# Turns and bias rows of the expert blocks done as pairs of 64-column fp32 products

## The chip, the cores and the metric

The kernel runs on one core of one Trainium2 chip. The metric is device time of one execution in microseconds (us), the median of several runs. Lower is better. The profile is one further execution, taken by the hardware profiler.

## The reference, cut to what matters

One layer of a decoder (a mixer of pooling, convolution and a recurrent unit, then a mixture of experts) is applied to 520 tokens of width 1024. The change lies in the mixture of experts:

```python
logits = (xt @ router_w + router_b)
top_v, top_i = lax.top_k(logits, TOP_K)          # 4 of 32 experts for each token
...
g = xblk @ w_gate[e] + b_gate[e]                 # 1024 x 1024 each, fp32
u = xblk @ w_up[e] + b_up[e]
g = jnp.minimum(g, SWIGLU_LIMIT)
u = jnp.clip(u, -SWIGLU_LIMIT, SWIGLU_LIMIT)
glu = g * jax.nn.sigmoid(SWIGLU_ALPHA * g)
((u + 1.0) * glu) @ w_down[e] + b_down[e]
...
y = jax.ops.segment_sum(yb * row_w[:, None], row_tok, num_segments=T + 1)[:T]
```

All 32 experts are visited. Each has three matrices of 4 MiB, so 384 MiB of weights are read from HBM in one execution.

## The kernel before, in words

The first 300 us or so compute the mixer, the router and the tables that say which tokens go to which expert. The rest, up to about 1298 us, is the loop over experts, `for s in range(E)` on each engine, and a tail that sums up the output.

**Blocks.** An expert has 64, 96, 128 or 160 places for tokens, by its rank in size: `WIDTH[s]` is 2 (20 experts), 3 (6 experts), 4 (4 experts) or 5 (2 experts). `BLOCKS` cuts them into blocks of 64 and 32 places: (64,), (64, 32), (64, 64), (64, 64, 32).

**Products (L1893 to L1898).** A block of 64 places uses the TensorE array as two halves of 64 columns. The places are the stationary operand, 512 columns of weights the moving one. Half 0 makes output columns 0 to 511 on partitions 0 to 63, half 1 makes 512 to 1023 on partitions 64 to 127, so that one PSUM bank holds 64 places by 1024 outputs. A block of 32 places uses four quarters of 32 columns in the same way, 256 moving columns each. Everything is plain fp32. In `project` a matrix takes four chunks of 1 MiB with two steps of 128 rows each, so a 64-place block makes 4 x 2 x 2 = 16 calls of `mm`.

**Other fp32 `mm` calls named below.** The router (L1823) makes 8 calls for a tile of 128 tokens: 128 columns of `h2T` stationary, 32 columns of `rw` moving. The conditioning products (L1626) put the 9 columns of `cT` on four column quarters, with 128 moving columns each, in 32 calls for a group.

**Bias rows (`bias`, L1884).** Each accumulation begins with the bias: `sel` (128x128, fp32r) has in its columns a one at the row of this expert's bias in `btab` (128x512, fp32r). For a 64-place block this is one product over the full 128 columns of the array. For a 32-place block it is four 32-column fp32 products (L1891).

**Turns.** The gathered rows (`xrow`, token by feature) are turned to feature by token by `turn_rows`, eight transposes of 128 columns with `ident` as moving operand (L1570). 24 gathers are turned, 16 of 128 rows, 6 of 96 and 2 of 32. The activations `act_t` are turned by `turn_act` before the down projection: 4 transposes for each 64-place block, 2 for each 32-place block, 168 in all. The banks of turned rows are copied to SBUF by ScalarE and VectorE.

**Order on TensorE, for each s.** Gate project, up project, turn of the rows of the next expert (where a new gather is due), down of expert s-1, turn of the activations of s.

**Loads.** SyncE loads the weights in order, in chunks of 1 MiB, into a ring of 18 buffers. A load waits until TensorE has finished with the chunk that lay in its buffer (`m_used`). All of it is in one hardware queue. Gathers (of `xrow`) and scatters (of the results) go through GpSimd.

Of the kernel before, what the change touches and what calls it, by code (L numbers as in the profile page):

```python
# [5 lines left out]
F32 = mybir.dt.float32  # L6
# [8 lines left out]
P = 128  # L15
D = 1024
KC = D // P
# [47 lines left out]
T_BANKS = (6, 7, 4)  # L65
# [49 lines left out]
def trunk_program(nc, x_prompt, x_sample, state_pool, state_conv, state_lru_conv, state_lru_h, c_prompt, c_sample,  # L115
# [36 lines left out]
    (hT_hi, hT_lo), W0 = place(A0, ("hT_hi", [P, KC, TOK], F32R), ("hT_lo", [P, KC, TOK], F32R))  # L152

    (oT, oS, _), OEND = place(A0, ("oT", [P, TT - 1, 2, KC, P], F32R), ("oS", [P, KC, NB], F32), ("oS_pad", [P, KC, NB], F32))
    assert OEND <= W0
    (scr1,), _ = place(A0, ("scr1", [P, D], F32))
# [67 lines left out]
    (acc, out_t, sq_e), T1 = place(0, ("acc", [P, 2, D], F32), ("out_t", [P, TT, D], F32), ("sq_e", [P, D], F32))  # L224
    (yrow_a,), G1 = place(A0, ("yrow_a", [P, 2, K, D], F32))
    (_, yrow_b), G2 = place(N0, ("xrow_pad", [P, 2, D], F32), ("yrow_b", [P, 3, K, D], F32))
    assert G2 <= M2
    TAIL = (TT - 1,) + tuple(range(TT - 1))
# [10 lines left out]
    with ctx:  # L239
        psum = ctx.enter_context(nc.psum_tensor("psum", [P, 8, 512], F32))  # L240
        bk = [psum[:, i, :] for i in range(8)]
# [314 lines left out]
        def _(g):  # L556
# [142 lines left out]
            for s in range(E):  # L699
                for n, _, _, _ in TURNS[s + 1]:  # L700
                    g.wait_ge(xt_ps, n + 1)
                    if n + 2 < ALL_TURNS:
                        gather(n + 2)
                if s:
                    scatter(s - 1)
# [854 lines left out]
        def _(pe):  # L1560
            mm = nc.tensor.matmul
# [7 lines left out]
            def turn(out, src, rows):  # L1569
                return nc.tensor.transpose(out, src, ident[0:rows, 0:rows])  # L1570
# [4 lines left out]
            for k in range(KC):  # L1575
                last = turn(bk[4][:, NC * k:NC * k + NC], c_all[:, k * P:k * P + P], NC)
# [60 lines left out]
            for m in range(16):  # L1637
                last = turn(bk[2][:, NC * m:NC * m + NC], modA[:, m * P:m * P + P], NC)
# [4 lines left out]
            for k in range(KC):  # L1643
                last = turn(bk[5][:, NB * k:NB * k + NB], x1[0:NB, TT - 1, k * P:k * P + P], NB)
            last.then_inc(xs_ps, 1)
            for k in range(KC):
                if k >= 2:
                    pe.wait_ge(h1_act, k - 1)
                for t in range(TT - 1):
                    last = turn(bk[3 + k % 2][:, t * P:t * P + P], x1[:, t, k * P:k * P + P], P)  # L1650
# [112 lines left out]
            for m in range(4):  # L1763
                turn(bk[1][0:11, m * P:m * P + P], x_lru[:, m, LB + SEQ - LB:LB + TOK], P)
                last = turn(bk[2][0:9, m * P:m * P + P], h_tail[:, m, :], P)
# [77 lines left out]
            for b in range(1, TT):  # L1843
                last = mm(bk[5][:, E * b:TT * E], ones_b[:, :], mask[:, 0:TT - b, :].rearrange("p t e -> p (t e)"),
                          start=False, stop=(b == TT - 1))
# [3 lines left out]
            for b in range(TT):  # L1849
                last = mm(bk[7][0:E, 256:256 + E], mask[:, b, :], ones_b[:, 0:E], start=(b == 0), stop=(b == TT - 1))  # L1850
# [3 lines left out]
            for e in range(2):  # L1854
                for t in range(TT):
                    last = mm(bk[1][0:FIRST, 2 * e:2 * e + 2], hot01[:, 2 * t + e, :], spots[:, t, :], start=(t == 0),
                              stop=(t == TT - 1))
# [7 lines left out]
            def find_rows():  # L1865
# [4 lines left out]
                              start=(i == 0), stop=(i == TT * K - 1))  # L1870
                last.then_inc(idx_ps, 1)

            def turn_rows(b, rows, full, evicted, count):

                pe.wait_ge(x_rows[b], full)
                if evicted is not None:
                    pe.wait_ge(aT_a, evicted)
                    pe.wait_ge(xg_a, count)
                    pe.wait_ge(xg_d, count)
                for k in range(KC):  # L1880
                    last = turn(bk[6 + k // 4][:, (k % 4) * P:(k % 4) * P + rows], xrow[0:rows, b, k:D:KC], rows)
                last.then_inc(xt_ps, 1)

            def bias(out, mat, w):  # L1884

                if w == 64:
                    mm(out, sel[:, :], btab[:, mat, :], start=True, stop=False)  # L1887
                else:
                    for g4 in range(4):
                        h, c = g4 // 2, 256 * (g4 % 2)  # L1890
                        mm(out[32 * g4:32 * g4 + 32, :], sel[:, 64 * h:64 * h + 32].bitcast(F32),  # L1891
                           btab[:, mat, c:c + 256].bitcast(F32), start=True, stop=False)
# [38 lines left out]
            def turn_act(widths):  # L1931

                for b, w in enumerate(widths):
                    for j in range(w // 16):
                        last = turn(bk[T_BANKS[b]][:, P * j:P * j + P], act_t[:, b, 256 * (j // 2) + j % 2:256 * (j // 2) + 256:2], P)
                    last.then_inc(at_ps, 1)

            def parts_of(s):
# [6 lines left out]
            def full_at(c0):  # L1945
                return lambda j: 16 * ((c0 + j) // NBUF + 1)

            turn_rows(0, GATHERS[0][1], 16, None, None)
            for s in range(E):
                c0, widths, before = first_chunk(s), BLOCKS[WIDTH[s]], blocks_before(s)  # L1950
                pe.wait_ge(sel_done, s + 1)
                pe.wait_ge(xg_a, turns_before(s))
                pe.wait_ge(xg_d, turns_before(s))
                if s >= 3:
                    pe.wait_ge(y_a, blocks_before(s - 2))
                project(0, [bank_of(G_BANKS, s, b) for b in range(len(widths))], widths, parts_of(s), c0, full_at(c0))
                if s == 0:
                    find_rows()
                if s >= 2:
                    pe.wait_ge(y_a, blocks_before(s - 1))  # L1960
                if s:
                    pe.wait_ge(aT_a, before)
                project(1, [bank_of(U_BANKS, s, b) for b in range(len(widths))], widths, parts_of(s), c0 + 4, full_at(c0 + 4))
                for n, _, rows, _ in TURNS[s + 1]:
                    turn_rows(n % 2, rows, 16 * (n // 2 + 1), before if before else None, n)
                if s == 1:
                    pe.wait_ge(tables_done, 1)
                if s:
                    pe.wait_ge(glu_done, before + len(widths))
                    down([down_bank(s - 1, b) for b in range(len(BLOCKS[WIDTH[s - 1]]))], BLOCKS[WIDTH[s - 1]],  # L1970
                         c0 + 8, full_at(c0 + 8))
                pe.wait_ge(act_done, before + len(widths))
                pe.wait_ge(xg_a, turns_before(s + 1))
                pe.wait_ge(xg_d, turns_before(s + 1))
                turn_act(widths)
            for t in range(TT):
                out = bk[0][0:E, t * P:t * P + P] if t < 4 else bk[1][0:E, 0:P]
                last = turn(out, wfull[:, t, :], P)
# [6 lines left out]
            def extra(q):  # L1985

                def full(c):
                    def count(j):
                        slot = (12 + c + j) % NBUF
                        return q * 16 + 16 * (-(-(12 * E - slot) // NBUF) + 1)  # L1990
                    return count

                pe.wait_ge(y_a, q * 2 + ALL_BLOCKS)
                turn_rows(0, P, q * 16 + 16 * (len(range(0, ALL_TURNS, 2)) + 1), q * 2 + ALL_BLOCKS, q + ALL_TURNS)
                pe.wait_ge(xg_a, q + (ALL_TURNS + 1))
                pe.wait_ge(xg_d, q + (ALL_TURNS + 1))
                pe.wait_ge(sel_done, q + (E + 1))
                both = [(xa, 0), (xa, 64)]
                project(0, (bk[4], bk[5]), (64, 64), both, 12, full(0))
                project(1, (bk[0], bk[1]), (64, 64), both, 16, full(4))  # L2000
                pe.wait_ge(act_done, q * 2 + (ALL_BLOCKS + 2))
                turn_act((64, 64))
                pe.wait_ge(aT_a, q * 2 + (ALL_BLOCKS + 2))
                down((bk[2], bk[3]), (64, 64), 20, full(8))
# [5 lines left out]
            def tail_out_banks(i):  # L2010

                return [bk[2 * (i % 4) + n][0:ROWS[TAIL[i]], :] for n in range(2)]
# [16 lines left out]
            for i, t in enumerate(TAIL):  # L2029
# [6 lines left out]
                for n in range(2):  # L2036
                    for j in range(BY_PE[i]):
                        last = mm(tail_out_banks(i)[n], diag[0:r, i, j, 0:r], yrow[i][0:r, j, 512 * n:512 * n + 512],
                                  start=False, stop=(j == BY_PE[i] - 1))
# [29 lines left out]
```

## Time and profile before

| | |
|---|---|
| median of 3 runs | 1357.33 us (1352.21 to 1359.2) |
| the profiled execution | 1352.83 us |
| its span in the profile | 1351.1 us |
| TensorE (PE) busy | 1256.2 us, 93% |
| TensorE weight load (PEld) busy | 560.7 us, 41% |
| VectorE, ScalarE, GpSimd busy | 21%, 15%, 8% |
| read from HBM | 470.26 MB |
| mean granted TensorE clock | 0.967 of full speed |

The busy time of TensorE is the union of its matmuls, each drawn with its pipeline latency, so that a run of matmuls is best measured from its start to the start of the next. "x64" behind a row is a count of instructions as the chip ran them.

### The profile page before, as it was taken

The page shows a single profiled execution, that of the slowest core. Times are in us where ns is not written, and L with a number is a line of the kernel's source. Part 1 is how long each engine was busy: PE and PEld are TensorE (multiplying, and loading weights), DVE is VectorE, ACT ScalarE, POOL GpSimd, SP SyncE. Part 2 cuts the span into 40 slices and gives each one's busy share as a digit, 9 for nine tenths or more (in the row PEclk, how much of TensorE's full clock was granted, in tenths as well). Part 3 has the DMA queues.
Part 4 walks back from the last instruction along what each step waited for, and adds up shares of the span by engine and source line. Part 5 has one row for each costly group of instructions (what it writes and reads, how often), then busy time and mean ns, then how long its engine had stood idle before and what let it go on. Part 6 is the DMA issues. An engine that isn't in the chain of part 4 may idle for free.

```text
span 1351.1 us, 19196 instructions
## 1 busy us (share of the span) xinstructions
PE 1256.2 (93%) x8190; PEld 560.7 (41%) x8190; DVE 287.0 (21%) x562; ACT 198.4 (15%) x347; POOL 110.4 (8%) x176
## 2 busy tenths in 40 slices
PE   2899977968999999999999999999999999999976
PEld 1686955843333333333333333333333333333322
DVE  0651585576100100000000000001001010001027
ACT  3513243220010000000000001001001000100012
POOL 3010022010000000100001100000001001000000
PEclk9999988968999999999999999999999999999978
DMA  9551479379999999999999999999999999999974
GB/s 317 194 160 32 156 246 350 138 312 403 348 403 420 421 422 421 408 409 422 407 407 420 420 415 421 421 420 403 419 417 420 421 421 421 420 422 421 422 299 183
DMA packets 95076, 486.43 MB, mean 360 GB/s; under 512 B 13649, under 2 KB 21852, under 8 KB 45302
## 3 DMA queue, kind: packets, MB, share of 16 engines
q1 hardware_dynamic: 83306, 461.15, 84.9%
q0 software_dynamic: 8608, 20.82, 4.1%
q10 hardware_dynamic: 3076, 3.22, 0.8%
q8 instruction: 66, 1.08, 0.3%
q14 instruction: 20, 0.16, 0.0%
HBM read 470.26 MB, written 18.04 MB: 361 GB/s over the span
## 4 chain that ended last, share of the span: by engine, by line
PE 81%; DMA 8%; DVE 5%; SPq 3%; ACTq 1%; ACT 1%; issue 1%; POOL 0%; DVEq 0%; POOLq 0%
PE psum L1897 61%; PE psum L1570 5%; PE psum L1565 3%; PE psum L1566 3%; PE psum L1567 3%; DMA raw<-in_moe_w_gate 2%; DMA raw<-in_moe_w_down 2%; SPq L481 2%; PE psum L1887 2%; DMA bd_x<-in_lru_wx 1%; ACTq L755 1%; PE psum L1719 1%; DMA raw<-in_w_out 1%; PE psum L2018 1%; DMA xrow<-h_scratch,gidx 1%
## 5 line engine op out<-in xcount | busy, mean ns | idle before, releaser
L1897 PE MATMUL psum<-raw,aT 128*64 128x512 f32 (+1 forms) x1728 | 301.2, 533 | 4.0 <-DMA raw<-in_moe_w_down 3.8
L1897 PE MATMUL psum<-raw,xb 128*64 128x512 f32 (+1 forms) x1920 | 304.0, 512 | 0.3 <-DMA raw<-in_moe_w_gate 0.3
L1897 PE MATMUL psum<-raw,xa 128*64 128x512 f32 x1280 | 283.5, 595 | 0.0
L1491 DVE TENSOR_SCALAR act_t<-psum 128x512 f32<-128x512 f32 (+1 forms) x46 | 28.4, 642 | 873.5 <-PE psum L1897 873.5
L1897 PEld LDWEIGHTS psum<-raw,xb 128*64 128x64 f32 (+1 forms) x1920 | 100.4, 126 | 189.0 <-issue 175.0
L1897 PEld LDWEIGHTS psum<-raw,aT 128*64 128x64 f32 (+1 forms) x1728 | 98.3, 129 | 187.8 <-issue 166.7
L1897 PEld LDWEIGHTS psum<-raw,xa 128*64 128x64 f32 x1280 | 88.2, 137 | 169.7 <-issue 169.7
L979 ACT ACTIVATE glu<-psum 128x512 f32<-128x512 f32 (+1 forms) x46 | 24.2, 559 | 291.6 <-PE psum L1897 291.6
L661 POOL DMA_INDIRECT xrow<-h_scratch,gidx x24 | 27.5, 1145 | 464.4 <-PE psum L1570 430.4
L1565 PE MATMUL psum<-hT_hi,w_hi 128*128 128x260 f32 x208 | 59.4, 286 | 0.0
L1566 PE MATMUL psum<-hT_lo,w_hi 128*128 128x260 f32 x208 | 58.9, 283 | 0.0
L1567 PE MATMUL psum<-hT_hi,w_lo 128*128 128x260 f32 x208 | 58.7, 282 | 0.0
L673 POOL DMA_INDIRECT y_scratch<-yst_a,sunit x23 | 22.9, 997 | 305.6 <-ACT yst_a L994 260.4
L994 ACT ACTIVATE yst_a<-psum 128x512 f32<-128x512 f32 (+1 forms) x27 | 14.5, 558 | 210.3 <-PE psum L1897 210.3
L1626 PE MATMUL psum<-raw,cT 128*9 128x128 f32 x768 | 33.2, 342 | 8.9 <-DMA raw<-in_ada_w 7.3
L1565 PEld LDWEIGHTS psum<-hT_hi,w_hi 128*128 128x128 f32 x208 | 39.1, 188 | 0.9 <-issue 0.8
L1567 PEld LDWEIGHTS psum<-hT_hi,w_lo 128*128 128x128 f32 x208 | 39.2, 189 | 0.0
L1566 PEld LDWEIGHTS psum<-hT_lo,w_hi 128*128 128x128 f32 x208 | 39.1, 188 | 0.1
L1570 PE MATMUL psum<-ident,xrow 128*128 128x128 f32 (+2 forms) x192 | 27.9, 290 | 9.2 <-DMA xrow<-h_scratch,gidx 9.2
L1887 PE MATMUL psum<-btab,sel 128*128 128x512 f32 x76 | 34.3, 477 | 1.1 <-ACT xb L1004 1.1
L1570 PEld LDWEIGHTS psum<-ident,xrow 128*128 128x128 f32 (+2 forms) x192 | 23.5, 198 | 28.0 <-issue 18.7
L1570 PEld LDWEIGHTS psum<-ident,act_t 128*128 128x128 f32 x168 | 22.5, 208 | 27.0 <-issue 25.2
(399 smaller groups left out, 923.6 us busy)
## 6 DMA issues: line engine op xcount, KB each, us to landing
raw<-in_moe_w_gate SPq DMA_DIRECT2D x128, 1024.0 KB, 26.3
raw<-in_moe_w_up SPq DMA_DIRECT2D x128, 1024.0 KB, 26.9
raw<-in_moe_w_down SPq DMA_DIRECT2D x128, 1024.0 KB, 26.8
raw<-in_ada_w SPq DMA_DIRECT2D x24, 1024.0 KB, 9.2
raw<-in_w_in SPq DMA_DIRECT2D x7, 1024.0 KB, 11.6
x<-in_x_prompt SPq DMA_DIRECT2D x2, 2048.0 KB
raw<-in_w_out SPq DMA_DIRECT2D x4, 1024.0 KB, 14.4
yrow_a<-y_scratch SPq DMA_DIRECT2D x2, 2048.0 KB, 10.6
```

The lines of the kernel that those rows point to most:

```text
L481: sp.dma_start(buf(slot).rearrange("p (k n) -> p k n", k=2), src).then_inc(m_full[slot], 16)
L661: g.indirect_dma_start(out=out, out_offset=None, in_=h2_d, in_offset=bass.IndirectOffsetOnAxis(ap=index, axis=0), bounds_check=h2_last, oo ...
L673: g.indirect_dma_start(out=out, out_offset=bass.IndirectOffsetOnAxis(ap=index, axis=0), in_=src, in_offset=None, bounds_check=last, oob_is ...
L979: ac.activation(glu[:, b, 0:bank.shape[1]], bank, ACT.Gelu_apprx_sigmoid).then_inc(glu_done, 1)
L1491: v.tensor_scalar(act_t[:, b, 0:bank.shape[1]], bank, 8.0, -6.0, ALU.min, ALU.max).then_inc(u_done, 1)
L1565: mm(out, lhi, rhi, start=start, stop=False)
L1566: mm(out, lhi, rlo, start=False, stop=False)
L1567: return mm(out, llo, rhi, start=False, stop=stop)
L1570: return nc.tensor.transpose(out, src, ident[0:rows, 0:rows])
L1626: last = mm(outs[j], cT[:, 4 * kh + k, :], raw[:, slot, 512 * k + P * j:512 * k + P * j + P], start=False, stop=(kh == 1 and k == 3))
L1887: mm(out, sel[:, :], btab[:, mat, :], start=True, stop=False)
L1897: last = mm(out[w * g4:w * g4 + w, :], x, weights[:, 8 * w * g4:8 * w * g4 + 8 * w], start=start, stop=stop)
```

## The change

Three kinds of full-width work in the expert loop are done as two 64-column products side by side, like the weights' own products. The transposes of gathered rows and of activations become ordinary fp32 products with the identity as moving operand. The bias row of a 64-place block becomes two products, with `sel` and `btab` read as fp32 instead of fp32r. The 32-place bias, `find_rows`, the turn of `wfull` at the end, and everything before the expert loop stay as they are.

```diff
+            def turn_halves(out, src, rows):
+
+                for h in range(2):
+                    last = mm(out[64 * h:64 * h + 64, :], src[:, 64 * h:64 * h + 64], ident[0:rows, 0:rows],
+                              start=True, stop=True)
+                return last
+
...
                 for k in range(KC):
-                    last = turn(bk[6 + k // 4][:, (k % 4) * P:(k % 4) * P + rows], xrow[0:rows, b, k:D:KC], rows)
+                    last = turn_halves(bk[6 + k // 4][:, (k % 4) * P:(k % 4) * P + rows], xrow[0:rows, b, k:D:KC], rows)
                 last.then_inc(xt_ps, 1)
...
                 if w == 64:
-                    mm(out, sel[:, :], btab[:, mat, :], start=True, stop=False)
+                    for h in range(2):
+                        mm(out[64 * h:64 * h + 64, :], sel[:, 64 * h:64 * h + 64].bitcast(F32),
+                           btab[:, mat, :].bitcast(F32), start=True, stop=False)
...
                     for j in range(w // 16):
-                        last = turn(bk[T_BANKS[b]][:, P * j:P * j + P], act_t[:, b, 256 * (j // 2) + j % 2:256 * (j // 2) + 256:2], P)
+                        last = turn_halves(bk[T_BANKS[b]][:, P * j:P * j + P],
+                                           act_t[:, b, 256 * (j // 2) + j % 2:256 * (j // 2) + 256:2], P)
                     last.then_inc(at_ps, 1)
```

## Rows read from the trace of the kernel before

**Rows 1.** The page: busy time of each engine, share of the span, instructions.

```profile
PE 1256.2 (93%) x8190; PEld 560.7 (41%) x8190; DVE 287.0 (21%) x562; ACT 198.4 (15%) x347; POOL 110.4 (8%) x176
```

**Rows 2.** Stretches: start:end, length, busy time of each engine, clock, DMA share, GB/s.

```profile
304.00:314.00 10.00, 5.99 (x25) 2.51 (x25) 9.45 (x18) 2.15 (x3) 0.00 (x0) 0.51 1.02 363
...
340.00:345.00 5.00, 5.00 (x54) 1.98 (x54) 0.00 (x0) 0.87 (x2) 0.00 (x0) 1.00 0.80 320
...
385.00:1280.00 895.00, 893.65 (x5102) 321.35 (x5100) 67.09 (x134) 76.47 (x146) 63.57 (x61) 1.00 1.01 418
```

**Rows 3.** Waits: who waited for whom, us in total, times, longest.

```profile
PE psum L1897 <- DMA raw<-in_moe_w_down: 3.8, 5, 1.1
...
SPq L481 <- PE psum L1897: 453.6, 230, 19.0
```

**Rows 4.** The page's costliest groups: line, engine, count, busy, mean ns.

```profile
L1570 PE MATMUL psum<-ident,xrow 128*128 128x128 f32 (+2 forms) x192 | 27.9, 290 | 9.2 <-DMA xrow<-h_scratch,gidx 9.2
L1887 PE MATMUL psum<-btab,sel 128*128 128x512 f32 x76 | 34.3, 477 | 1.1 <-ACT xb L1004 1.1
...
L1570 PEld LDWEIGHTS psum<-ident,act_t 128*128 128x128 f32 x168 | 22.5, 208 | 27.0 <-issue 25.2
```

**Rows 5.** PE in order of time: start, length, group (4-wide, then 2-wide expert).

```profile
800.06 13.95 PE L1897 MATMUL psum<-raw,xb 128*64 128x512 f32 x64
813.94 0.73 PE L1887 MATMUL psum<-btab,sel 128*128 128x512 f32 x2
814.60 13.95 PE L1897 MATMUL psum<-raw,xb 128*64 128x512 f32 x64
828.49 1.16 PE L1570 MATMUL psum<-ident,xrow 128*128 128x128 f32 x8
829.58 11.12 PE L1897 MATMUL psum<-raw,aT 128*64 128x512 f32 x96
840.63 1.23 PE L1570 MATMUL psum<-ident,act_t 128*128 128x128 f32 x8
841.61 0.48 PE L1887 MATMUL psum<-btab,sel 128*128 128x512 f32 x1
842.02 7.09 PE L1897 MATMUL psum<-raw,xa 128*64 128x512 f32 x32
849.04 0.49 PE L1887 MATMUL psum<-btab,sel 128*128 128x512 f32 x1
849.46 7.09 PE L1897 MATMUL psum<-raw,xa 128*64 128x512 f32 x32
856.48 1.06 PE L1570 MATMUL psum<-ident,xrow 32*128 32x32 f32 x8
857.47 2.80 PE L1897 MATMUL psum<-raw,aT 128*64 128x512 f32 x12
```

**Rows 6.** Weight loads (PEld) in order of time inside such a product run.

```profile
810.41 0.14 PEld L1897 LDWEIGHTS psum<-raw,xb 128*64 128x64 f32 x2 [0.28 <-issue]
...
812.99 0.14 PEld L1897 LDWEIGHTS psum<-raw,xb 128*64 128x64 f32 x2 [0.28 <-issue]
```

**Rows 7.** PE in order of time: small-column groups of other stages, at full clock.

```profile
188.90 1.93 PE L1626 MATMUL psum<-raw,cT 128*9 128x128 f32 x64
190.76 0.40 PE L1620 MATMUL psum<-adab,bsel 12*9 12x128 f32 x8
...
255.68 1.87 PE L1823 MATMUL psum<-rw,h2T 128*128 128x32 f32 x16
257.38 1.07 PE L1570 MATMUL psum<-ident,h2f 128*128 128x128 f32 x8
```

**Rows 8.** PE in order of time: a 3-wide expert's bias, turn of 96 rows.

```profile
701.08 0.64 PE L1891 MATMUL psum<-btab,sel 128*32 128x256 f32 x8
...
712.70 1.13 PE L1570 MATMUL psum<-ident,xrow 96*128 96x96 f32 x8
713.75 6.53 PE L1897 MATMUL psum<-raw,aT 128*64 128x512 f32 x52
```

## The prediction

> **What bounds the kernel now.** I read the page first: PE is busy 93% of the span, no other engine over 41% [rows 1]. Then the stretches: from 385 to 1280 us, which is nearly the whole expert loop, PE is busy 893.65 of 895 us and at the same time the DMA engines are at a share of 1.01 with 418 GB/s [rows 2]. Two resources are full at once, and the question is which has slack. The waits tell: PE waits for weights 3.8 us in all, in five waits, while SyncE waits 453.6 us for PE to give buffers back [rows 3]. Last, the order of time: a 64-instruction product run takes 13.88 us from its start to the start of what follows, both times that it stands there [rows 5], and its weight loads come every 0.43 us to the hundredth (six steps in 2.58 us) [rows 6], so no wait hides inside the busy time. The reader should see that each side has a slack of a few us only: if TensorE's work shrinks, the loads stay the limit. If it grows, everything over 3.8 us goes into the end.
>
> **How many instructions a call is.** An ordinary fp32 `mm` is two instructions on PE, a transpose or an fp32r product one. The router's 8 calls stand as x16 and the 32-place bias's 4 calls as x8 [rows 7, 8], and the 16 calls of a 64-place project as x32, while 8 transposes are x8 and one fp32r bias is x1 [rows 5]. A pair of halves with 512 moving columns takes 0.429 us [rows 6]; a call on both halves is two such pairs.
>
> **Bias rows.** 76 before [rows 4]. 52 stand alone (40 for the 2-wide experts, 12 for the 3-wide ones), and one takes 0.42 us from its start to the product's (849.04 to 849.46). 24 come by twos (4- and 5-wide experts), 0.66 us for both (813.94 to 814.60) [rows 5]. After: 4 instructions of 64x512 for each, two pairs of 0.429, so 0.86 us. That adds 52 x 0.44 = 22.9 and 12 x (1.72 - 0.66) = 12.7, in all 35.6 us. fp32r streams its moving columns twice as fast and in one instruction; all that is given up. The new shape is that of the products beside it, so this term is firm.
>
> **Turns.** Before, eight transposes of `xrow` take 1.09 us (828.49 to 829.58) and with 96 rows 1.05, with 32 rows 0.99; eight of `act_t` take 0.98 (840.63 to 841.61) [rows 5, 8]. So 16 x 1.09 + 6 x 1.05 + 2 x 0.99 = 25.7 us for 24 gathers (192 transposes) [rows 4] and 168 x 0.1225 = 20.6 for the activations [rows 4], 46.3 in all. After: 360 turns x 2 halves x 2 instructions = 720 pairs. No row shows a pair of 64 columns with 128 moving. The nearest is L1626: four column quarters, 128 moving, 64 instructions in 1.86 us, 0.116 for each group of four with the change of mode in it [rows 7]; a quarter of the products' 0.429 gives 0.107. From the side of the loads, the router's fp32 instructions with 128 stationary columns and only 32 moving come every 0.106 us (1.70 / 16) [rows 7]. Two loads of 64 columns can hardly cost more than one of 128, whether they run together or in turn. I take 0.111 for the 592 pairs with 128 moving columns (16 gathers and all activations), 0.10 for the 96 pairs of the 96-row gathers, 0.08 for the 32 pairs of the 32-row ones: 65.7 + 9.6 + 2.6 = 77.9, so +31.6 us. Lower bound, streaming alone: 592 x 0.107 + 96 x 0.082 + 32 x 0.055 = 73.0, +26.7. Upper bound 0.120 for all 720, a little above what the strided transposes of `act_t` show (0.1225, and those load 128 columns): 86.4, +40.1.
>
> **The mode changes that go.** A product run of 64 is 32 pairs x 0.429 = 13.73 us, and takes 13.88 where full-width work follows: 0.15 for leaving the 64-column shape and coming back. There are 88 such visits (32 for the up bias, 32 for turns of activations and gate bias together, 24 for gathered rows). The 16 bias visits of the 3- and 5-wide experts still go on to a 32-column bias, so that I count 0.05 there: 72 x 0.15 + 16 x 0.05 = 11.6 us saved. The Trainium skill ("TensorEngine Tiling (Array Packing)", Key Properties) says that changing the tiling mode drains TensorE, which speaks for the change; the trace agrees, with this 0.15. The same page (Restrictions) says that column tiling shuts out the transpose mode for fp32, and "FP8 and Floating Point Precision" (TensorE Precision Notes) counts four passes for a true fp32 product, which speaks against it: as an estimate from these two pages alone a turn of 128 rows costs 4 x 128 cycles, 0.21 us, and the sum comes out near the lower bound.
>
> **The start.** The first gather's turn and the first bias fall into a stretch with a granted clock of 0.51, the lower level of 1.2 GHz [rows 2], while all the rest runs at 1.00, the level of 2.4 GHz. Their added time, 0.3 and 0.4 us as counted, is about twice as long there: +0.8 us.
>
> **The sum.** 35.6 + 31.6 - 11.6 + 0.8 = +56.4 us of TensorE. All of it is in order on the engine that never rests, and it lies beside nothing. The only cover is the 3.8 us in which PE waited for weights: with later buffer releases the loads go on ahead and these waits vanish. That leaves +52.6. With the bounds of the turns, +47.7 to +61.1. What is late next: SyncE's loads wait for PE longer, DMA falls below its full share, GpSimd's scatters follow later, and the tail starts 53 us later, unchanged. ScalarE and VectorE copy the turns out later but their results are wanted only after a project or a down of 7 us or more, except at the very first expert. The profiled execution, 1352.8, becomes 1405.4. The median of the runs before is 4.5 us above it. Runs of before are held by the memory as much as by TensorE, and those of after by TensorE alone, so I do not carry the 4.5 over in full: 1406.
>
> **The rivals.**
> *Loads that do not overlap.* If the load of each half had to wait for the matmul in flight, a pair would cost its 0.107 and about half of the router's 0.106, some 0.165, and 720 pairs 118.8 us: +41 on my sum, 1447. Against it: in the product run two loads start together every 0.43 us right in the middle of the matmul run [rows 5, 6], and transposes come every 0.1225 though their loads alone take 208 ns from start to end [rows 4]. The Trainium skill ("TensorE: Matmul & The Clock Gate", Part 3) has the rule that loads overlap with matmuls in flight only where the row groups differ; here both halves use all rows. The trace doesn't agree with that rule. But at 128 moving columns the overlap would have to be nearly perfect, and no row has this shape, so the rival keeps 7 in 100.
> *One instruction for each half, and a cover by the loads: no slower.* If products with the identity and with `sel` were one instruction each at these same rates, the new work would be half: 38.9 for the turns against 46.3, 76 x 0.43 = 32.6 for the bias rows against 29.8, less 11.6 for the modes: TensorE wins 16 us. Then the loads decide, and nearly nothing comes of it: between 340 and 380 us the DMA engines have some idle time (share 0.80 in one stretch [rows 2]), which earlier buffer releases could fill by 1 or 2 us. 1356, no change. It decides as soon as the added TensorE time is under 3.8 us. Against it stands the count x8 for four calls of the fp32 bias. 4 in 100.
> *TensorE's growth hidden in part.* The ring of 18 buffers could hide growth only where PE now waits, and it waits 3.8 us. For a result of 1380 PE would have to hold waits that the profile doesn't show. 3 in 100.
>
> **Chances and range.** Within 0.5% (6.8 us) is about what a measurement of this kernel can tell from no change. The forecast has 86 in 100, the rivals 7, 4 and 3. The forecast's own bounds give 1400 to 1414; with 3 or 4 us for the median's own scatter on either side and the mis-sized mode changes (0.10 or 0.20 instead of 0.15 moves the sum by 3.6 each way), 1395 to 1421. Slower 0.95, same 0.04, faster 0.01.
>
> **What would show it.** In the profile after: L1887 gone as 128*128 x76 and there as 128*64 x304, turns as 128*64 with 1440 instructions or near; 0.86 us from a lone bias to its product; 1.75 to 1.8 us for eight turns of 128 rows; product runs at 13.73 instead of 13.88; no wait of PE for weights after 385 us; DMA share near 0.96 instead of 1.01. The prediction is wrong if eight turns take 2.6 us (loads exposed), or if the bias has two instructions instead of four, or if PE busy grows as said and the end does not move.

## The result, and the profile after

The change makes the kernel slower: 1405.43 us (median of 4 runs, 1402.97 to 1408.31) against 1355.14 us before (4 runs, 1352.21 to 1359.2). The ratio is 1.0381, with a 95% interval of 1.0346 to 1.0416, so +50 us. Forecast were 1406 us and a range of 1395 to 1421. The profiled execution of the changed kernel took 1408.31 us (span 1406.6), the longest of its four runs, and that of before, 1352.83, is nearly the shortest of its own. Their difference of 55.5 us is therefore a few us larger than that of the medians.

The page of the changed kernel shows more busy time on PE and PEld alone, beside [rows 1]:

```profile
PE 1317.0 (94%) x9498; PEld 619.2 (44%) x9498; DVE 288.1 (20%) x562; ACT 199.8 (14%) x347; POOL 108.4 (8%) x176
...
L1895 PE MATMUL psum<-btab,sel 128*64 128x512 f32 x304 | 77.1, 599 | 1.1 <-ACT xb L1004 1.1
...
L1876 PE MATMUL psum<-ident,xrow 128*64 128x128 f32 (+2 forms) x768 | 51.2, 287 | 8.8 <-DMA xrow<-h_scratch,gidx 8.8
...
L1876 PE MATMUL psum<-ident,act_t 128*64 128x128 f32 x672 | 42.2, 273 | 0.9 <-DVE xb L1504 0.9
```

The counts are those of "two halves, two instructions each": 76 bias rows became 304 instructions, 192 and 168 transposes became 768 and 672.

In the order of time, the same experts as in [rows 5] (a 4-wide one, then a 2-wide one):

```profile
833.06 13.90 PE L1906 MATMUL psum<-raw,xb 128*64 128x512 f32 x64
846.79 1.89 PE L1895 MATMUL psum<-btab,sel 128*64 128x512 f32 x8
848.51 13.90 PE L1906 MATMUL psum<-raw,xb 128*64 128x512 f32 x64
862.24 2.12 PE L1876 MATMUL psum<-ident,xrow 128*64 128x128 f32 x32
864.19 11.07 PE L1906 MATMUL psum<-raw,aT 128*64 128x512 f32 x96
875.08 1.92 PE L1876 MATMUL psum<-ident,act_t 128*64 128x128 f32 x32
876.83 1.03 PE L1895 MATMUL psum<-btab,sel 128*64 128x512 f32 x4
877.69 7.04 PE L1906 MATMUL psum<-raw,xa 128*64 128x512 f32 x32
...
892.38 2.11 PE L1876 MATMUL psum<-ident,xrow 32*64 32x32 f32 x32
894.42 5.80 PE L1906 MATMUL psum<-raw,aT 128*64 128x512 f32 x26
```

Read each row from its start to the next start. Two bias rows take 1.72 us (846.79 to 848.51; 0.66 before), one takes 0.86 (0.42). Eight turns of 128 gathered rows take 1.95 (1.09), eight of activations 1.75 (0.98), and eight turns of only 32 rows take even 2.04 (0.99). A product run of 64 takes 13.73 instead of 13.88: the mode changes around it are gone.

The waits and the stretch that answers to [rows 2, 3]:

```profile
PE psum L1876 <- DMA xrow<-h_scratch,gidx: 8.8, 1, 8.8
PE psum L2028 <- ACT diag L1034: 3.4, 1, 3.4
PE psum L1895 <- ACT xb L1004: 1.1, 1, 1.1
PE psum L1876 <- DVE xb L1504: 0.9, 1, 0.9
```

```profile
385.00:1280.00 895.00, 895.00 (x5966) 351.17 (x5964) 61.92 (x123) 73.69 (x139) 61.34 (x60) 1.00 0.99 399
```

No wait for weights is left among PE's waits, PE is busy for all of the 895 us, and 399 GB/s are moved where it was 418.

Where the time went can be summed from the starts of all matmuls between the first turn and the last down product, each interval given to the instruction that opens it (us). The last digits are rounded, so a column can be off by 0.1:

| | before | changed kernel | difference | the prediction's term |
|---|---|---|---|---|
| 64-place bias rows | 29.9 | 67.9 | +38.0 | +35.6, and 0.4 of the start |
| turns of gathered rows | 29.2 | 49.7 | +20.5 | +14.9, and 0.4 of the start |
| turns of activations | 20.8 | 36.8 | +16.0 | +16.7 |
| 64-column weight products | 809.4 | 791.5 | -17.8 | -11.6 modes, -3.8 waits |
| all else | 101.1 | 100.8 | -0.3 | 0 |
| whole stretch | 990.4 | 1046.8 | +56.4 | +52.6 |

Ahead of this stretch the profiled execution of the changed kernel was some 3 us later, and its tail 3 to 4 us shorter.

### The profile page after: what moved, and what is told of

It is laid out like the page before. It is cut to its first block, busy times and chain, and to the rows that moved or that the text cites. A ratio compares the mean times of both kernels' runs of the same rounds, so it can differ in the third digit from the quotient of the medians.

```text
span 1406.6 us, 21812 instructions
## 1 busy us (share of the span) xinstructions
PE 1317.0 (94%) x9498; PEld 619.2 (44%) x9498; DVE 288.1 (20%) x562; ACT 199.8 (14%) x347; POOL 108.4 (8%) x176
## 4 chain that ended last, share of the span: by engine, by line
PE 88%; DVE 5%; DMA 3%; ACTq 1%; issue 1%; ACT 1%; SPq 1%; DVEq 0%; POOLq 0%
PE psum L1906 63%; PE psum L1876 6%; PE psum L1895 5%; PE psum L1565 3%; PE psum L1566 3%; PE psum L1567 3%; DMA bd_x<-in_lru_wx 1%; PE psum L1719 1%; ACTq L755 1%; DMA raw<-in_w_out 1%; PE psum L1570 1%; PE psum L2028 1%; PE psum L1900 1%; DMA xrow<-h_scratch,gidx 1%; SPq L442 1%
## 5 line engine op out<-in xcount | busy, mean ns | idle before, releaser
L1906 PEld LDWEIGHTS psum<-raw,xb 128*64 128x64 f32 (+1 forms) x1920 | 101.1, 126 | 189.5 <-issue 177.1
L1906 PEld LDWEIGHTS psum<-raw,xa 128*64 128x64 f32 x1280 | 91.9, 137 | 182.7 <-issue 182.7
L1895 PE MATMUL psum<-btab,sel 128*64 128x512 f32 x304 | 77.1, 599 | 1.1 <-ACT xb L1004 1.1
L1876 PEld LDWEIGHTS psum<-ident,xrow 128*64 128x64 f32 (+2 forms) x768 | 51.0, 213 | 21.3 <-issue 12.4
L1876 PE MATMUL psum<-ident,xrow 128*64 128x128 f32 (+2 forms) x768 | 51.2, 287 | 8.8 <-DMA xrow<-h_scratch,gidx 8.8
L1876 PEld LDWEIGHTS psum<-ident,act_t 128*64 128x64 f32 x672 | 38.9, 139 | 18.7 <-issue 17.7
L1876 PE MATMUL psum<-ident,act_t 128*64 128x128 f32 x672 | 42.2, 273 | 0.9 <-DVE xb L1504 0.9
```

The lines of the kernel that those rows point to most:

```text
L1876: last = mm(out[64 * h:64 * h + 64, :], src[:, 64 * h:64 * h + 64], ident[0:rows, 0:rows], start=True, stop=True)
L1895: mm(out[64 * h:64 * h + 64, :], sel[:, 64 * h:64 * h + 64].bitcast(F32), btab[:, mat, :].bitcast(F32), start=True, stop=False)
L1906: last = mm(out[w * g4:w * g4 + w, :], x, weights[:, 8 * w * g4:8 * w * g4 + 8 * w], start=start, stop=stop)
```

## Experiments

Medians and ratios are against the kernel before on the same chip: 1353.85 us (15 runs) for the first four, 1353.22 us (13 runs) for the last three. "Loop" is the whole stretch of the table above, from the kernel's own trace.

### One part at a time

**bias_only**: the changed kernel with both kinds of turns put back.

```diff
-                    last = turn_halves(bk[6 + k // 4][:, (k % 4) * P:(k % 4) * P + rows], xrow[0:rows, b, k:D:KC], rows)
+                    last = turn(bk[6 + k // 4][:, (k % 4) * P:(k % 4) * P + rows], xrow[0:rows, b, k:D:KC], rows)
...
-                        last = turn_halves(bk[T_BANKS[b]][:, P * j:P * j + P],
-                                           act_t[:, b, 256 * (j // 2) + j % 2:256 * (j // 2) + 256:2], P)
+                        last = turn(bk[T_BANKS[b]][:, P * j:P * j + P], act_t[:, b, 256 * (j // 2) + j % 2:256 * (j // 2) + 256:2], P)
```

> Only the bias rows of the 64-place blocks are done as two fp32 halves; the turns stay transposes. Theory (TensorE's own time goes to the end of the run): bias rows add 35.6 us, 4.0 us of mode changes go (only the up biases stand between 64-column products), 0.4 us more at the start, and 3.8 us of waits for weights vanish: +28 us. Rival (the ring of buffers hides a growth of this size): under +10 us.

Measured: 1385.87 us, ratio 1.0239 (1.0212 to 1.0265), +32 us; loop +34.8. The rival is out. The loop grew by 6.6 us more than the expected 28 (28.2 as added up). Most of it is the seam between turns and bias. With the bias in another shape than the turns before it, the turns of activations take 26.4 us in all, and 20.8 before: 5.6 more, 0.175 for each of the 32 experts. The bias rows, at 70.3 us in all, are 4.5 above their expected growth of 36.0, and the products gave back 11.4 where 7.8 was expected.

**rows_only**: of the change, `turn_rows` alone. Against the kernel before:

```diff
-                    last = turn(bk[6 + k // 4][:, (k % 4) * P:(k % 4) * P + rows], xrow[0:rows, b, k:D:KC], rows)
+                    last = turn_halves(bk[6 + k // 4][:, (k % 4) * P:(k % 4) * P + rows], xrow[0:rows, b, k:D:KC], rows)
```

> Only the turns of gathered rows are done as fp32 halves. With the turn times of the changed kernel's trace (about 1.95 us for eight, where the prediction had 1.78): 24 x 1.96 - 25.7 = +21.3, less 3.6 for the mode changes of 24 visits, plus 0.3, less 3.8 of vanished waits: +14 us. By the prediction's own price of a pair (0.111, 0.10, 0.08) it would be +8 us. Rival (hidden by the ring): under +3 us.

Measured: 1361.95 us, ratio 1.0063 (1.0045 to 1.0082), +8 us; loop +11.2. Turns of gathered rows took 49.8 us (49.7 in the changed kernel), +20.5, while the 64-column products fell by 9.0. That is more than the 3.6 of mode changes and 3.8 of waits; the part on why the prediction was right takes it up. The median agrees with the lower of the two expected numbers, but not for its reason: the price of a turn is the higher one.

**acts_only**: of the change, `turn_act` alone. Against the kernel before:

```diff
-                        last = turn(bk[T_BANKS[b]][:, P * j:P * j + P], act_t[:, b, 256 * (j // 2) + j % 2:256 * (j // 2) + 256:2], P)
+                        last = turn_halves(bk[T_BANKS[b]][:, P * j:P * j + P],
+                                           act_t[:, b, 256 * (j // 2) + j % 2:256 * (j // 2) + 256:2], P)
```

> Only the turns of the activations are done as fp32 halves. 336 pairs x 0.109 - 20.6 = +16.0 us; no mode change goes, since the gate bias behind them is still full-width; less 3.8 us of vanished waits: +12 us. Rival (hidden by the ring): under +3 us.

Measured: 1364.01 us, ratio 1.0064 (1.0043 to 1.0086), +10 us by the medians and +9 by the ratio; loop +11.4. The size is as expected, but "no mode change goes" was only half of it: a mode change moved. The product runs before the turns end 3.1 us earlier in all, since halves follow them. The same 3.1 us come back at the seam to the full-width bias, where the turns take 39.9 us in all and 36.8 in the changed kernel. So turns and seam cost 19.1 us more than the 20.8 of before, and the products 8.0 us less.

The three parts add up to 32.0 + 8.1 + 10.2 = 50.3 us by the medians, the size of the whole change. The loops add up to 57.4 against 56.4. Each part alone, though, already used up the waits, which makes the sum too small, and bias_only and acts_only each leave a seam between shapes that the whole doesn't have, which makes it too large. These two nearly cancel.

### The other direction: less work for TensorE

**before_no_bias**: the kernel before without the bias products of 64-place blocks.

```diff
                 if w == 64:
-                    mm(out, sel[:, :], btab[:, mat, :], start=True, stop=False)
+                    pass
...
-                                                    False, j == 3 and kk == 1)
+                                                    w == 64 and j == 0 and kk == 0, j == 3 and kk == 1)
```

> The kernel before without the bias products of the 64-place blocks: their first weight product starts the accumulation, so that those blocks lack b_gate and b_up. TensorE's work shrinks by 52 x 0.42 + 12 x 0.66 + 4.0 of mode changes = 33.8 us. Theory (weights come at the full rate of the DMA engines already, so a smaller TensorE cannot help): 0 to -4 us, and PE waits for weights of some 30 us appear. Rival (TensorE alone is the bound): -34 us.

Measured: 1348.85 us, ratio 0.9957 (0.9931 to 0.9982), -5 us; loop -1.6 (988.8). All 29.9 us of bias rows are gone, and the loop is nearly as long as it was. PE's waits of this kernel say where they went:

```profile
PE psum L1897 <- DMA raw<-in_moe_w_down: 15.1, 19, 2.6
...
PE psum L1897 <- DMA raw<-in_moe_w_up: 5.4, 11, 0.6
...
PE psum L1897 <- DMA raw<-in_moe_w_gate: 1.9, 3, 0.9
```

22.4 us of waits for weights stand in place of 4.1 before (the 3.8 of [rows 3] and 0.3 more for gate weights). The products' intervals, with these waits in them, grew by 23.1 us. Another 5.5 us went to the seam behind the turns of activations (26.3 us in all, 20.8 before), as in bias_only. So TensorE's own work shrank by less than the expected 33.8 us, and the waits are fewer than the expected 30. A smaller TensorE buys next to nothing here, while a larger one costs what it grows by, less the waits of before. The run is a little faster than the expected 0 to -4 us. What is over the loop's 1.6 us lies ahead of the loop (1.1 us) and in the tail (1.9) of the profiled run, and I can't explain it by the change.

### Halves or plain fp32: which of them costs?

**bias_full_fp32**: the kernel before with one full-width fp32 product for a bias row.

```diff
-                    mm(out, sel[:, :], btab[:, mat, :], start=True, stop=False)
+                    mm(out, sel[:, :].bitcast(F32), btab[:, mat, :].bitcast(F32), start=True, stop=False)
```

> The kernel before with the bias of the 64-place blocks as one full-width fp32 product (two instructions) in place of fp32r. Theory (the price is that of plain fp32: two instructions, each at half the columns per cycle; halving the width costs nothing): a lone bias takes 0.86 us and the run is 30 to 36 us longer than before, as with halves. Rival (the halves are what costs): no change from before.

**bias_b_halves**: halves again, but of one instruction each. The biases are cut to bf16, which changes what is computed.

```diff
-                    mm(out, sel[:, :], btab[:, mat, :], start=True, stop=False)
+                    sel_b, tab_b = sel[:, :].bitcast(BF16)[:, 1::2], btab[:, mat, :].bitcast(BF16)[:, 1::2]
+                    for h in range(2):
+                        mm(out[64 * h:64 * h + 64, :], sel_b[:, 64 * h:64 * h + 64], tab_b, start=True, stop=False)
```

> The kernel before with the bias of the 64-place blocks as two halves again, but reading the upper 16 bits of sel and btab as bf16 (the biases are cut to 8 bits): one instruction for each half. Theory: one pair of 0.22 us for a bias instead of two of 0.43; bias rows take some 17 us instead of 29.8, TensorE's work shrinks by 10 to 15 us, but the weights do not come faster: 0 to -5 us. Rival (TensorE alone is the bound): -10 to -15 us. A second rival (any work in 64-column halves is slow): slower than before.

Measured: bias_full_fp32 1394.51 us, ratio 1.0307 (1.0278 to 1.0335), +41 us; loop +44.1. bias_b_halves 1352.82 us, ratio 0.9996 (0.9979 to 1.0012), no difference; loop -0.2. A lone up bias and the product behind it, first full-width fp32, then bf16 halves:

```profile
875.84 1.12 PE L1887 MATMUL psum<-btab,sel 128*128 128x512 f32 x2
876.89 7.09 PE L1897 MATMUL psum<-raw,xa 128*64 128x512 f32 x32
```

```profile
848.11 0.40 PE L1889 MATMUL psum<-btab,sel 128*64 128x512 bf16 x2
848.34 7.04 PE L1899 MATMUL psum<-raw,xa 128*64 128x512 f32 x32
```

1.05 us against 0.23, with 0.42 for the fp32r bias of before and 0.86 for fp32 halves. So the halves are not what costs: at one instruction each they are the cheapest form of all. Full-width fp32 is dearer than fp32 in halves, 76.1 us of bias rows in all against 67.9. Its run came out 5 us above the expected 30 to 36, because the expectation took 0.86 us for a lone bias and had no price for the changes of shape around it. Behind 64-column products its first matmul takes 0.53 us up to the second, behind transposes 0.43; its second takes 0.52 us up to the product, where in halves the last pair takes 0.42.

Plain fp32 costs. A bf16 half is one instruction, an fp32 half two, and the two pairs of the fp32 halves take 0.86 us where the one bf16 pair takes 0.23. For fp32r the mixer of the kernel before shows the rate, first with one fp32r matmul of 260 columns, then with plain fp32 ones:

```profile
126.08 0.28 PE L1567 MATMUL psum<-hT_hi,w_lo 128*128 128x260 f32 x1
126.20 1.04 PE L1708 MATMUL psum<-W,bd_a 128*128 128x260 f32 x4
127.08 1.04 PE L1708 MATMUL psum<-W,bd_x 128*128 128x260 f32 x4
```

That is 0.12 us from start to start against 0.22 for each of the four (0.88 / 4).

In bias_b_halves TensorE gave back 9.7 us of bias rows (20.1 in all, where some 17 was expected), and 5.8 went to the seam behind the turns of activations. The mode changes around the products gave another 5.2, so that TensorE's own work shrank by 9.1 us. The products still grew by 3.8, since 9.0 us more of waiting stands in their intervals; 10.0 us of waits for weights are in the trace. The rival by which TensorE alone decides is out once more: 9.1 us less work, and a loop 0.2 us shorter.

### The dearer turns of gathered rows

**rows_contig**: the changed kernel with contiguous columns as stationary operand. The features come out permuted.

```diff
-                    last = turn_halves(bk[6 + k // 4][:, (k % 4) * P:(k % 4) * P + rows], xrow[0:rows, b, k:D:KC], rows)
+                    last = turn_halves(bk[6 + k // 4][:, (k % 4) * P:(k % 4) * P + rows], xrow[0:rows, b, k * P:k * P + P], rows)
```

> The changed kernel, but each half's stationary operand is a contiguous run of columns of the gathered rows (k * 128 on) instead of every eighth: the features come out in another order, so the gate and up products are of permuted rows. Theory (the load of 64 columns with a step of 32 bytes sets the 0.121 us of a pair, not the streaming of 128 columns): eight turns of 128 rows fall from 1.95 to 1.75 us like those of the activations, those of 32 rows from 2.04 to 1.0 or less, and the loop is 8 to 12 us shorter than the changed kernel's. Rival (the time of a pair has another cause, such as the 96 or 32 moving columns or the banks): no change.

Measured: 1398.79 us, ratio 1.0339 (1.0311 to 1.0367), against 1.0381 of the changed kernel. That is about 6 us less, though the two intervals overlap a little. The trace decides: loop 1038.9 against 1046.8, and of these 7.8 us (just short of the expected 8 to 12) the turns of gathered rows account for 7.5 (42.3 against 49.7). The eight turns of 32 rows in this kernel:

```profile
885.38 1.12 PE L1876 MATMUL psum<-ident,xrow 32*64 32x32 f32 x32
886.43 13.95 PE L1906 MATMUL psum<-raw,aT 128*64 128x512 f32 x64
```

And the weight loads of the turns, first of the changed kernel, then of rows_contig:

```profile
L1876 PEld LDWEIGHTS psum<-ident,act_t 128*64 128x64 f32 x672 | 38.9, 139 | 18.7 <-issue 17.7 <-DVE act_t L1498 1.1
L1876 PEld LDWEIGHTS psum<-ident,xrow 128*64 128x64 f32 x512 | 33.9, 212 | 8.2 <-issue 8.2
...
L1876 PEld LDWEIGHTS psum<-ident,xrow 32*64 32x64 f32 x64 | 4.0, 211 | 1.6 <-issue 1.6
```

```profile
L1876 PEld LDWEIGHTS psum<-ident,xrow 128*64 128x64 f32 x512 | 29.1, 137 | 9.1 <-issue 9.1
...
L1876 PEld LDWEIGHTS psum<-ident,xrow 32*64 32x64 f32 x64 | 2.0, 133 | 1.6 <-issue 1.6
```

A load of 64 columns takes 212 ns when its elements stand 32 bytes apart, 139 ns at 8 bytes and 137 ns side by side. Eight turns of 32 rows take 2.04 us with the wide step and 1.05 without (0.128 and 0.066 a pair), and eight of 96 rows 1.90 and 1.32. With 128 moving columns the wide step costs less, 1.95 against 1.74 us (855.44 to 857.18 in the trace of rows_contig). The edit changes only which columns a turn reads, and with that the step, so it is the load with the wide step that holds the pairs back. Inside a visit they then come every 0.12 us whether 32, 96 or 128 columns move. Without it the pace follows the moving columns: 0.059, 0.082 and 0.109 us.

## Why the prediction was right, point by point

- **Both resources full, and which gives way.** Shown from both sides. With 29.9 us of TensorE's work left out the loop lost 1.6 us and waits of 22.4 us appeared; in every kernel with more work on TensorE the loop grew and the waits for weights went.
- **Two instructions for an fp32 `mm`.** Shown by the counts, x304, x768 and x672, and by the bias in its four forms. This was the step on which the sign hung. With one instruction per half, in bf16, the change to the bias rows is worth nothing at all (0.9996), as the second rival said of a kernel with one instruction for each half.
- **Bias rows, +35.6 us.** Measured +38.0, with the start in it, where 36.0 were counted. A lone bias is 0.86 us as said. The rest is the first bias, at the lower clock of 1.2 GHz (granted clock 0.50 from 313 to 316 us; 1.90 us against 0.70), and the 3- and 5-wide experts, where a bias of 32 columns follows and 0.10 us of the change of shape is counted here: at 753.18 us in the trace of the changed kernel a lone bias takes 0.96 us up to the 32-column one.
- **Turns of activations, 0.111 a pair.** Measured 0.109 (1.75 us for 16 pairs), +16.0 against +16.7.
- **Turns of gathered rows, +14.9 us.** This term was sized too small: +20.5, where 15.3 were counted with the start. The step that failed is the one that takes 0.111 us from the streaming side for all 128-column pairs and less for fewer rows. With the step of 32 bytes the load sets the pace, at 0.122 a pair for 128 rows (1.95 / 16) where 0.111 was taken, 0.119 for 96 rows (1.90 / 16) where it was 0.10, and 0.128 for 32 rows where it was 0.08. Two of the six visits of 96 rows also lie in the first stretch of the loop and took 2.66 and 2.89 us before, where the prediction counted 1.05, and 3.96 and 2.99 in the changed kernel. The forecast of 1.75 to 1.8 us for eight turns of 128 rows was missed at 1.95. The upper bound of 0.120 was too low for two of the three sizes. The prediction calls it a little above the 0.1225 of the transposes of `act_t`, but it lies below that. "Two loads of 64 columns can hardly cost more than one of 128" was also wrong at this step: 0.128 a pair against 0.124 for a transpose of 32 rows before.
- **Mode changes and waits, -15.4 us.** Measured -17.8 on the 64-column products. Lined up interval by interval with the kernel before, 8.3 us of it stand at the ends of the product runs (0.52 us before full-width work, 0.42 before halves) and 3.7 in the first two pairs behind such work. These 12.0 us answer to the 11.6. The intervals that hold the five waits for down weights are 4.7 us shorter, where the row of waits says 3.8: each wait costs some 0.17 us more than its idle time. The same 4.7 us stand in rows_only. The remaining 1.1 us lie scattered, 0.4 of them in a product that ran while the clock rose.
- **The cancelling.** The two misses in cost (+5.2 for gathered rows, +2.0 for bias rows), the larger gain on the products (-2.4), the turns of activations (-0.7) and all else (-0.3) leave the loop 3.8 us above the forecast. The median of the runs, 1405.43, lies on the 1406 by luck, because the 55.5 us of the profiled pair are 5 us more than the medians differ by. The hit is better than the sum deserves.
- **DMA share near 0.96.** It was 0.99 over the same stretch, so this sign was missed. The bytes per time fell as the share was to fall, 418 to 399 GB/s. Why the share did not, no run here shows.
- **Loads that do not overlap (first rival).** Out for the turns of activations, at 0.109 a pair, and out for those of gathered rows too, whose 0.12 to 0.13 stays under the rival's 0.165. The trace of the changed kernel doesn't agree with the rule of the Trainium skill ("TensorE: Matmul & The Clock Gate", Part 3) that stood beside it: both halves use all rows, and their loads overlap with the matmuls in flight.

## What to carry to other kernels

Count instructions, not calls. A transpose or an fp32r bias traded for plain fp32 halves became four instructions in place of one. A turn of the activations went from 0.12 to 0.22 us, a lone bias from 0.42 to 0.86, and the saved change of mode (0.15 us a visit here) didn't pay for that. Where two resources are full at once, price growth and shrinkage apart: here 30 us of bias rows left out brought next to nothing, and what TensorE's work grew by was paid in full but for some 5 us of waits. When a stationary operand is read with a step, look at the duration of its weight load: with a step of 32 bytes it set the pace here, with little loss at 128 moving columns (0.122 us a pair against 0.109) and nearly twice the time at 32 (0.128 against 0.066).

## What the runs showed of the hardware that I had not expected

- A load of 64 fp32 columns takes 212 ns with a step of 32 bytes and 137 to 139 ns with 4 or 8. The full-width transposes of before gave no sign of it: with a step of 32 bytes their loads took 194 ns and they came every 0.11 us, with one of 8 bytes 208 ns and every 0.12. Why the step matters to the one form and not to the other, no run here shows.
- A change of shape costs different amounts by what stands on its two sides. From the last transpose to a full-width fp32r bias it is 0.04 us from start to start, to a full-width fp32 bias 0.12, and to a 64-column bias 0.21. The last is about 0.18 us more than the first (5.6 us in 32 experts in bias_only, 5.8 in bias_b_halves).
